# State-space groups: squares on ScalarE and a one-column product per group, in place of a running sum on GpSimd

## What is computed

```python
def mamba2_ssd(h, w_in, conv_w, conv_b, dt_bias, a_log, d_skip, norm_g, w_out):
    zxbcdt = h @ w_in
    z, xbc, dt = jnp.split(zxbcdt, [SSM_D_INNER, SSM_D_INNER + SSM_CONV_DIM], axis=-1)
    xbc = jax.nn.silu(_causal_dwconv(xbc, conv_w, conv_b))
...
    y = _ssd_scan(xs, dt, a, bm, cm)
    y = y + xs * d_skip.reshape(SSM_GROUPS, rep)[..., None].astype(xs.dtype)
    y = y.reshape(bsz, seq, SSM_D_INNER)
    y = rmsnorm(y * jax.nn.silu(z), norm_g)
    return y @ w_out
```

## Time and profile before

| | |
|---|---|
| median of 3 runs | 1547.66 us (1545.26 to 1547.70) |
| profiled execution, time | 1547.53 us |
| its span, first to last instruction | 1545.8 us |
| TensorE busy | 1508.5 us, 98% |
| VectorE busy | 1222.4 us, 79% |
| ScalarE busy | 1020.5 us, 66% |
| GpSimd busy | 97.9 us, 6% |
| granted TensorE clock, mean | 0.991 |

### The profile page before, as it was taken

One profiled execution on the slowest core, in us unless ns is written; L12 is line 12 of the kernel. 1 busy time (PEld: TensorE's weight loads), 2 busy tenths in 40 slices (PEclk: granted clock), 3 DMA queues, 4 the chain that ended last, 5 costly groups with the idle time before them and its releaser, 6 DMA issues.

```text
span 1545.8 us, 21011 instructions
## 1 busy us (share of the span) xinstructions
PE 1508.5 (98%) x7550; PEld 1263.7 (82%) x7550; DVE 1222.4 (79%) x1008; ACT 1020.5 (66%) x905; POOL 97.9 (6%) x115
## 2 busy tenths in 40 slices
PE   8899999999899999999999999999999999999997
PEld 7688888888889788788888888888888888888885
DVE  6665554456689858898898898898898998998996
ACT  5554444345688637777777777777777777777774
POOL 2042000000012214000000000000000000000020
PEclk9899999999999999999999999999999999999999
DMA  9369755545443438999999999999999999999997
GB/s 326 113 232 413 264 188 190 191 137 165 135 137 117 146 106 333 403 391 395 370 366 410 359 372 410 361 385 396 359 384 389 371 385 385 371 392 385 405 386 298
DMA packets 166229, 476.21 MB, mean 308 GB/s; under 512 B 9152, under 2 KB 35024, under 8 KB 166176
## 3 DMA queue, kind: packets, MB, share of 16 engines
q1 hardware_dynamic: 157152, 446.73, 77.7%
q0 software_dynamic: 5888, 19.23, 3.2%
q10 hardware_dynamic: 3136, 9.54, 1.5%
HBM read 454.49 MB, written 20.97 MB: 308 GB/s over the span
## 4 chain that ended last, share of the span: by engine, by line
PE 82%; issue 11%; DVE 2%; POOLq 1%; DMA 1%; ACT 1%; DVEq 1%; SPq 0%; POOL 0%; ACTq 0%
PE bank L781 26%; PE bank L783 26%; PE bank L782 26%; PE bank L1237 2%; DMA ring<-swa_w_qkv_in 1%; POOLq L395 1%; DVE w_lo L1354 1%; POOLq L393 0%; PE bank L1224 0%; PE bank L1001 0%; PE bank L806 0%; ACT w_hi L455 0%; PE bank L1292 0%; PE bank L1190 0%; PE bank L1213 0%
## 5 line engine op out<-in xcount | busy, mean ns | idle before, releaser
L1751 DVE TENSOR_TENSOR w_lo<-ring,w_hi 128x2048 fp32r<-128x2048 f32 x336 | 763.3, 2290 | 79.3 <-PE bank L783 73.1
L675 ACT ACTIVATE w_hi<-ring 128x2048 fp32r<-128x2048 f32 x336 | 635.7, 1919 | 141.3 <-DMA ring<-moe_w_gu_in 93.5
L781 PE MATMUL bank<-w_hi,xgT_hi 128*128 128x512 f32 x896 | 351.1, 392 | 3.4 <-DVE w_lo L1751 2.3
L783 PE MATMUL bank<-w_hi,xgT_lo 128*128 128x512 f32 x896 | 349.0, 390 | 0.0
L782 PE MATMUL bank<-w_lo,xgT_hi 128*128 128x512 f32 x896 | 348.6, 389 | 0.0
L1354 DVE TENSOR_TENSOR w_lo<-ring,w_hi 128x2048 fp32r<-128x2048 f32 (+1 forms) x84 | 194.9, 2323 | 116.0 <-ACT w_hi L455 115.2
L455 ACT ACTIVATE w_hi<-ring 128x2048 fp32r<-128x2048 f32 (+1 forms) x84 | 158.9, 1896 | 123.3 <-PE bank L783 116.6
L781 PEld LDWEIGHTS bank<-w_hi,xgT_hi 128*128 128x128 f32 x896 | 168.2, 188 | 38.0 <-DVE w_lo L1751 2.8
L783 PEld LDWEIGHTS bank<-w_hi,xgT_lo 128*128 128x128 f32 x896 | 168.2, 188 | 35.2
L782 PEld LDWEIGHTS bank<-w_lo,xgT_hi 128*128 128x128 f32 x896 | 168.3, 188 | 34.2
L781 PE MATMUL bank<-w_hi,m_hT_hi 128*128 128x512 f32 x448 | 175.8, 392 | 0.0
(11 more groups left out here) (337 smaller groups left out, 1634.4 us busy)
## 6 DMA issues: line engine op xcount, KB each, us to landing
ring<-moe_w_gu_in SPq DMA_DIRECT2D x230, 1024.0 KB, 7.0
ring<-moe_w_down_in SPq DMA_DIRECT2D x112, 1024.0 KB, 7.1
ring<-ffn_w_gu_in SPq DMA_DIRECT2D x28, 1024.0 KB, 6.7
ring<-ffn_w_down_in SPq DMA_DIRECT2D x14, 1024.0 KB, 4.8
xg_rows<-zeros POOLq DMA_DIRECT2D x36, 256.0 KB, 12.6
ring<-ssm_w_in_in SPq DMA_DIRECT2D x8, 1024.0 KB, 5.1
ring<-ssm_w_in_in SPq DMA_DIRECT2D x16, 512.0 KB, 3.9
ring<-ssm_w_in_in SPq DMA_DIRECT2D x32, 256.0 KB, 4.4
```

Source lines behind the costliest of these rows:

```text
L675: act.activation(w_hi[:, c % HI], ring[:, c % RING], ACT.Copy).then_inc(hi_ready, 1)
L781: pe.matmul(o, stat[0], mov[0], start=start, stop=False)
L783: return pe.matmul(o, stat[1], mov[0], start=False, stop=stop)
L1751: dve.tensor_tensor(w_lo[:, c % SPLIT], ring[:, c % RING], w_hi[:, c % HI].bitcast(F32), ALU.subtract).then_inc(lo_ready, 1)
```

## The change

ScalarE squares `yg_T` into a tile of its own, `squares`, right behind `yT_hi`, and raises `c_sq`. From the second group on it first waits for `c_norm`, that the group before has been summed. TensorE sums each group by four products with one column of ones into two columns of bank 5 that belong to that group, one stage later, behind y of the next group; the last group's stand where line 1173 stood. VectorE sums the eight pairs of columns with one reduction. GpSimd's loop and the memset of `sq_acc` are gone, `yg_T` is no longer overwritten by its square, and VectorE's wait for `c_sq` now is one for ScalarE.

```diff
--- before.py
+++ after.py
@@ -205,10 +205,10 @@
         f_hT_hi, f_hT_lo = phase(f_hT_hi=((KF, T), F32R), f_hT_lo=((KF, T), F32R))
         f_sg, f_hh = xs[:, 0].rearrange("p (t n) -> p t n", t=TT), xs[:, 1].rearrange("p (t n) -> p t n", t=TT)
 
-        z, _, acc, Xdt, arg, yg_T, sq_acc, XC_last, U = phase(
+        z, _, acc, Xdt, arg, yg_T, squares, XC_last, U = phase(
             z=((G, TT, 256), F32), under_yT_lo=((KI, T), F32), acc=((4, T), F32),
             Xdt=((TT, REP * 64), F32), arg=((3, REP, P), F32), yg_T=((2, T), F32),
-            sq_acc=((2, T), F32), XC_last=((4, T), F32), U=((4, T + 3), F32))
+            squares=((2, T), F32), XC_last=((4, T), F32), U=((4, T + 3), F32))
 
         XC = [xs[:, 0].rearrange("p (a b) -> p a b", b=T), xs[:, 1].rearrange("p (a b) -> p a b", b=T), XC_last]
 
@@ -385,14 +385,6 @@
                 for a in range(2):
                     pool_e.dma_start(y_rows[i][:, 512 * a:512 * (a + 1)], zeros[:]).then_inc(rows_cleared, 16)
             pool_e.wait_ge(rows_cleared, 2 * (3 * E + 3) * 16)
-            pool_e.wait_ge(c_pad, 1)
-            pool_e.memset(sq_acc, 0.0)
-            for g in range(G):
-                pool_e.wait_ge(c_yTsb, 2 * g + 2)
-                pool_e.tensor_tensor(yg_T, yg_T, yg_T, ALU.mult)
-                pool_e.drain()
-                pool_e.tensor_tensor(sq_acc, sq_acc, yg_T, ALU.add).then_inc(c_sq, 1)
-                pool_e.drain()
             pool_e.wait_ge(rows_ready, TT)
             pool_e.wait_ge(r_slots, 1)
             for t in range(TT):
@@ -653,6 +645,9 @@
                     for k in range(2):
                         act.activation(yT_hi[:, 2 * g + k], yg_T[:, k], ACT.Copy,
                                        scale=vT[:, 32 + 2 * g + k:33 + 2 * g + k]).then_inc(c_yThi, 1)
+                    if g >= 1:
+                        act.wait_ge(c_norm, g)
+                    act.activation(squares, yg_T, ACT.Square).then_inc(c_sq, 1)
                 if s < G:
                     ahead(GR0 + 2 * s + 4)
                 g = s - 1
@@ -1086,6 +1081,15 @@
             def out_product(c, tiles=range(TT)):
                 pe.wait_ge(c_yTsb, 2 * c + 2)
                 return times_rows(SO0, (yT_hi, yT_lo), c, KI, tiles)
+
+            def square_sums(g):
+
+                pe.wait_ge(c_sq, g + 1)
+                for t in range(TT):
+                    for k in range(2):
+                        ins = pe.matmul(bank[5][:, 3 * P + 2 * g + t:3 * P + 2 * g + t + 1],
+                                        squares[:, k, t * P:(t + 1) * P], ones[:, 0:1], start=(k == 0), stop=(k == 1))
+                ins.then_inc(c_norm, 1)
 
             def cross_decay(g):
                 pe.wait_ge(c_exp0, 2 * g + 1)
@@ -1132,6 +1136,8 @@
                             ins = pe.matmul(o[:, P:T], Xdt[:, 1, r * 64:(r + 1) * 64], arg[:, 1, r],
                                             start=False, stop=True)
                     ins.then_inc(c_y, 1)
+                    if g >= 1:
+                        square_sums(g - 1)
                 g = s - 1
                 if 0 <= g < G:
 
@@ -1167,12 +1173,7 @@
             for c in (3, 4):
                 out_product(c)
             out_product(5)
-            pe.wait_ge(c_sq, G)
-            for t in range(TT):
-                for k in range(2):
-                    ins = pe.matmul(bank[6][:, t:t + 1], sq_acc[:, k, t * P:(t + 1) * P], ones[:, 0:1],
-                                    start=(k == 0), stop=(k == 1))
-            ins.then_inc(c_norm, 1)
+            square_sums(G - 1)
             out_product(6, (0,))
             out_product(7, (0,)).then_inc(so_first, 1)
             out_product(6, (1,))
@@ -1738,8 +1739,9 @@
                     dve.tensor_tensor(arg[:, 2], arg[:, 2], cb, ALU.mult).then_inc(c_m, 1)
             ahead(MOE0 - 1)
 
-            dve.wait_ge(c_norm, 1)
-            dve.tensor_copy(st[:, 4, 0:2], bank[6][:, 0:2])
+            dve.wait_ge(c_norm, G)
+            dve.tensor_reduce(st[:, 4, 0:2], bank[5][:, 3 * P:3 * P + 2 * G].rearrange("p (g t) -> p t g", t=TT),
+                              AXX, ALU.add)
             dve.drain()
             i = root(4, DI, st[:, 4], c_var, c_sqrt, 1, 1)
```

## The result

The changed kernel takes 1550.53 us (median of 14 runs, 1548.18 to 1558.58) against 1547.47 (14 runs, 1545.13 to 1549.83): a ratio of 1.0026, 95% interval [1.0015, 1.0038], so 3.1 us slower. Its profiled execution spans 1549.1 us, that of before 1545.8.

A forecast was written before the change was run, and what follows sets the result against it. ScalarE's gapless 16.07 us loop was taken to bound the state-space groups, TensorE's 15.91 close behind. Terms 1.68 + 1.34 + 0.17 = +3.2 us on the profiled 1547.53 gave 1550.7, range 1547.6 to 1552.8.

The forecast's parts named there:

- Square, 6 x 0.53 = 3.18: In ScalarE's gapless loop, between yT_hi and the weight copy: squares of groups 0 to 5 add 0.53 us each, +3.18.
- What GpSimd gave back, 1.02 + 0.27 + 0.21 = 1.50: VectorE without GpSimd beside it: slow taps -1.02 us, a late TensorE's longer tap wait -0.27, taps held by a subtraction -0.21.
- The slowed subtractions were worth nothing: Five VectorE subtractions lose 0.84 us each beside GpSimd; recovering that gains nothing in ScalarE's loop, since VectorE then waits for ScalarE.
- The rival of the released VectorE: VectorE, not ScalarE, sets the start of the taps, so all 5.6 us that GpSimd cost returns: 1541.9 us; chance 0.04.
- with an unchanged wait for U: Sign at VectorE's convolution taps: they start every 16.6 us, their wait for ScalarE's U unchanged, behind a square of about 0.6.
- not fully: GpSimd's reads block VectorE's two-input SBUF operations only partly: 0.84 us lost, against 1.04 and more under an exclusive lock.
- y(6) later by 1.68: TensorE's product y of group 6, at 523.15 us, moves by 3.18 - 1.02 - 0.27 - 0.21 = +1.68 us.
- The deficit of 0.12 a stage, met by TensorE's saved waits: TensorE's loop 16.72 us against ScalarE's 16.60: 0.5 in four stages, met by TensorE's saved waits for slowed subtractions.
- Blocks behind y(6), 0.81 - 0.28 + 0.81, and 0.17 for semaphores: 1.51: On TensorE after 523.15 us: group 5's block less its Xdt wait, plus group 6's, +1.34 us; semaphore issue +0.17.
- Eight instructions at 0.10 us each, against the smaller price: TensorE's one-column block priced 0.81 us from the trace, not 0.65 by the skill, which gives about 0.3 less in sum.
- The rest: VectorE's reduction of 16 values, and GpSimd's memset and drains, lie behind 555 us beside TensorE's remaining products: nothing.
- The rival in which one-column products decide: At 1.12 us a block, TensorE's loop is 17.03 against ScalarE's 16.60: up to +4.8 us, or 1552.1; chance 0.15.

The follow-up runs named there:

- e1: Changed kernel without the squares and seven of the eight one-column blocks, GpSimd still idle; ratio 0.9995 to the kernel before.
- e2: Changed kernel with the square kept behind yT_hi on ScalarE, groups added up on VectorE, one one-column block at the end; ratio 1.0027 to the kernel before.
- e3: Changed kernel with ScalarE's square one stage later, ahead of Silu, groups added up on VectorE, one block at the end; ratio 0.9992, repeated 0.9986, to the kernel before.
- e7: Changed kernel with groups added up on VectorE, one block at the end, and ScalarE's weight copy moved ahead of the wait before yT_hi; ratio 0.9997 to before.
- e5: Changed kernel with every block of one-column products issued twice, except the last; ratio 1.0056 to the kernel before.
- e8: Changed kernel with only ScalarE's weight copy moved from behind yT_hi and the square to ahead of the wait before yT_hi; ratio 1.0016 to the kernel before.
- e6: Changed kernel with a second square of the same size on ScalarE for groups 0 to 6; ratio 1.0054 to the kernel before.
- e9: Kernel with VectorE sum and moved weight copy, plus twelve unread products in TensorE's idle time before y of group 6; ratio 0.9990 to the kernel before.
- e10: Changed kernel with the square twice, plus twelve unread products in TensorE's idle time before y of group 6; one execution, 1553.75 us, no ratio.

## Why the prediction was right

Forecast +3.2 us on the profiled execution, measured +3.3 between the spans, +3.06 between the medians and +3.48 in the stretch. The mechanism was right; part of the closeness is luck. The stretch is 0.29 above the terms, which add up to 3.19: -0.06 for the squares, +0.04 for GpSimd, +0.12 for TensorE's loop, +0.19 for the blocks behind y(6). The spans and medians hide that, as the 0.55 us ahead and the -0.73 behind nearly cancel. And a forecast right on the bound of what can be told could not choose between slower and the same. Its steps:

- **Square, 6 x 0.53 = 3.18.** The periods say 0.51 a stage (16.58 - 16.07), and from e1 to e2 y(6) comes 3.12 later after the taps of stage 2 (97.81 against 94.69). Right, and for the reason given: the square stands in a loop without a gap. e3 shows it from the other side.
- **What GpSimd gave back, 1.02 + 0.27 + 0.21 = 1.50.** e1's stretch is 1.51 shorter, 1.46 of it by y(6), and its taps show the three pieces as 1.01, 0.27 and 0.19. The slowed subtractions were worth nothing, as said: VectorE's wait for U went from 0.61 to 1.45. The rival of the released VectorE falls. But the sign "with an unchanged wait for U" was wrong, and against the prediction's own account: time saved ahead of a wait lengthens it. Two readings of GpSimd's rows were off too, with no effect on the sum. The addition beside the slow taps took 1.40 us, not the 3.14 of the earlier trace rows, which is another group's. And GpSimd's square, 488.14 to 489.18, shared at most 0.99 us with the subtraction that began at 488.19 and lost 0.84, with GpSimd's spans rough, so "not fully" is more than these rows can say. GpSimd's addition beside that subtraction took 3.14 and the one that VectorE waited for 1.26, so it was slowed as well:

```profile
445.02 1.40 POOL L394 TENSOR_TENSOR sq_acc<-sq_acc,yg_T 128x512 f32<-128x512 f32 x1 [5.31 <-issue]
...
523.43 1.26 POOL L394 TENSOR_TENSOR sq_acc<-sq_acc,yg_T 128x512 f32<-128x512 f32 x1
```

- **y(6) later by 1.68.** It came 523.15 - 427.00 = 96.15 us after the taps of stage 2 and now comes 97.93 after: +1.78. The 0.1 more is the next point.
- **The deficit of 0.12 a stage, met by TensorE's saved waits.** It was 0.17, since a block costs TensorE 0.84 among the groups and not 0.81 (0.88 if its own work is e7's 15.87), and the cover lasted three stages of four: taps at 494.01 were 0.13 late. With e2, which has no blocks there, y(6) comes 97.81 after the taps of stage 2, so blocks cost 0.12 up to y(6) in the changed kernel. As the prediction says, if that cover goes it shows in full; e5 and e8 show it gone.
- **Blocks behind y(6), 0.81 - 0.28 + 0.81, and 0.17 for semaphores: 1.51.** Measured 32.68 - 30.98 = 1.70. Here one sub-term failed. I took off 0.28 because TensorE had waited that long for VectorE's Xdt and would come later by itself. But Xdt in turn waited 0.80 us for TensorE's transposes (line 1159, the row of 529.50), and these stand behind the block: the block pushes the awaited work as well, TensorE still waited 0.19, and only 0.09 was saved. A block costs 0.90 there (18.80 us from y(7) to the last block against 17.90), so 0.90 - 0.09 + 0.90 = 1.71.
- **Eight instructions at 0.10 us each, against the smaller price.** The Trainium skill, TensorE: Matmul & The Clock Gate, section "Back-to-back issue gap", gives about 81 ns for a pair of 128 columns, by which estimate a block would take 0.65 us; the rows here show 0.84 and 0.90, so the measurement decides for the larger price. By the smaller one the sum would have been near the edge of what can be told from no change.
- **The rest.** No table load was added, `c_norm` was never waited for, and VectorE's reduction lies beside TensorE's products. The rival in which one-column products decide had the right mechanism, TensorE's loop becoming the longer, but needed 1.12 us a block.

## What to carry to other kernels

Find the loop, not the busy engine: an engine that was idle for 2.8 of 16 us made each stage 0.51 us longer by an instruction of 0.62, because it stood in the loop that had no gap; in that engine's idle time the same instruction cost nothing. Before moving work between engines write down the length of every loop, for behind one at 16.07 the next stood at 15.91, and easing one alone gives back less than it seemed to cost: of the changed kernel's stretch 1.98 us with ScalarE's loop eased (e8), 1.91 with the blocks gone (e2), and 5.01 with both (e3). A wait is shortened by a delay only if what it waits for does not stand behind the same delay.

## What the hardware showed that I had not expected

TensorE's idle time can cost more than itself. Around a wait of 2.65 us (e6) and of 2.13 us (e7) before y(6) its granted clock fell to 0.50; the windows of 3 us that hold the fall show 0.68 to 0.75. y(6)'s products took up to 1.12 us and not 0.65, and the delay to the end of the stretch was 1.4 to 1.6 us. With that wait filled with products that nobody reads, the profiles show no fall, and all of that was back behind y(6) (e9, e10); in e9 the filling itself cost 0.5 us ahead of y(6). The same length of wait did not do it in two other kernels, and falls elsewhere differ between executions of one kernel, so it has to be looked for in each trace.
